# Router of a hybrid diffusion layer: a memset and a cast moved, one top-k replacement dropped, half of a modulation on another engine, gate rows copied earlier

## What is computed

```python
mod = silu(cond) @ w_mod + b_mod                       # sh1, sc1, g1, sh2, sc2, g2
mixed = (gate_a * (o_a @ w_up_a) + gate_b * (o_b @ w_up_b)) @ w_out
x = layer_norm(ALPHA * x + g1 * mixed, ln1_g, ln1_b)
u = layer_norm(x) * (1.0 + sc2) + sh2                  # modulated by set: samples, prompt
probs = softmax(u @ w_router)                          # 16 experts
aff, idx = top_k(swapaxes(probs, 1, 2), cap)           # cap 64 of samples, 16 of prompt
xs = u[idx]
hid = silu(xs @ w_gate) * (xs @ w_up)
x = layer_norm(ALPHA * x + g2 * scatter_add(hid @ w_down * aff), ln2_g, ln2_b)
```

## Time and profile before

| what | us |
|---|---|
| median of 3 runs | 1477.09 (1476.99 to 1477.68) |
| the profiled execution | 1476.4 |
| its span | 1474.6 |
| TensorE busy | 1371.4 (93%) |
| VectorE busy | 620.1 (42%) |
| ScalarE busy | 249.5 (17%) |
| GpSimd busy | 71.3 (5%) |
| mean granted TensorE clock | 0.973 |

### The profile page before, as it was taken

The page is one execution under the profiler, slowest core; times in us unless marked ns, Lnnn a source line. Parts: engine busy times, 40 slices in busy tenths (PEclk is TensorE's granted clock), DMA queues, the critical chain, the costliest instruction groups (busy, mean ns, idle before and its releaser), DMA issues.

```text
span 1474.6 us, 24328 instructions
## 1 busy us (share of the span) xinstructions
PE 1371.4 (93%) x10632; PEld 753.1 (51%) x10632; DVE 620.1 (42%) x1358; ACT 249.5 (17%) x479; POOL 71.3 (5%) x63
## 2 busy tenths in 40 slices
PE   6999999998999999999999984999999999999991
PEld 2455555657888885666755441334334334334330
DVE  6222137546666662543332774222233222222336
ACT  4311122234222332110110022000100000001000
POOL 0000000000000000000000001111111111111110
PEclk9999999999999999999999996999999999999995
DMA  9822221410000000430132055999999999999974
GB/s 387 348 104 114 81 76 71 172 56 18 2 2 2 2 17 0 171 142 31 57 129 86 30 228 216 350 393 392 397 400 403 400 396 395 398 397 387 402 304 153
DMA packets 32028, 298.93 MB, mean 203 GB/s; under 512 B 3435, under 2 KB 7659, under 8 KB 15580
## 3 DMA queue, kind: packets, MB, share of 16 engines
q1 hardware_dynamic: 20876, 270.93, 45.7%
q0 software_dynamic: 7680, 17.11, 4.6%
q10 hardware_dynamic: 3408, 9.96, 1.7%
HBM read 280.69 MB, written 17.30 MB: 202 GB/s over the span
## 4 chain that ended last, share of the span: by engine, by line
PE 64%; DVE 5%; DMA 1%; issue 1%; ACT 0%; DVEq 0%; POOLq 0%
PE bank L570 62%; PE bank L991 1%; DVE hbuf L1884 1%; DVE front L1654 0%; DVE hbuf L2034 0%; DVE stats L2032 0%; PE bank L997 0%; DVE front L1999 0%; DMA hbuf<-y_dram 0%; DMA y_dram<-front,misc 0%; DMA front<-u_dram,misc 0%; DVE misc L1935 0%; PE bank L511 0%; DVE misc L1933 0%; DVE front L1936 0%
## 5 line engine op out<-in xcount | busy, mean ns | idle before, releaser
L570 PE MATMUL bank<-ring,front 128*32 128x256 f32 (+3 forms) x3312 | 430.6, 458 | 2.2 <-DVE front L1990 2.2
L570 PE MATMUL bank<-front,ring 128*128 128x128 f32 (+3 forms) x1416 | 402.9, 443 | 6.9 <-DVE front L1843 3.0
L570 PEld LDWEIGHTS bank<-front,ring 128*128 128x128 f32 (+1 forms) x1416 | 223.3, 189 | 187.0 <-issue 163.8
L570 PEld LDWEIGHTS bank<-ring,front 128*32 128x32 f32 (+3 forms) x3312 | 177.2, 124 | 248.6 <-issue 211.2
L570 PE MATMUL bank<-front 128*64 128x512 f32 (+4 forms) x3008 | 288.4, 355 | 4.4 <-DVE front L1714 2.4
L570 PEld LDWEIGHTS bank<-front 128*128 128x128 f32 (+3 forms) x3008 | 170.1, 141 | 107.5 <-issue 79.4
L2014 DVE TENSOR_TENSOR front<-bank,front 128x512 f32<-128x512 f32 x16 | 11.1, 692 | 275.2 <-PE bank L570 275.2
L1999 DVE STREAM_TRANSPOSE front<-front 32x256 f32<-32x256 f32 x192 | 83.4, 434 | 5.5
L1443 DVE SCALAR_TENSOR_TENSOR front<-bank,pk,front 128x511 f32<-128x511 f32 x64 | 32.2, 545 | 99.4 <-ACT front L1078 98.8
L1654 DVE COPY_PREDICATED front<-ck,bank 128x256 f32<-128x256 uint32 (+1 forms) x120 | 52.8, 443 | 25.3 <-PE bank L570 22.9
L1270 ACT ACTIVATE front<-bank 128x512 f32<-128x512 f32 x16 | 9.6, 597 | 291.6 <-PE bank L570 291.6
(11 more groups left out here) (290 smaller groups left out, 988.8 us busy)
## 6 DMA issues: line engine op xcount, KB each, us to landing
ring<-w_e_gate_dram SPq DMA_DIRECT2D x32, 2048.0 KB, 15.5
ring<-w_e_up_dram SPq DMA_DIRECT2D x32, 2048.0 KB, 14.5
front<-w_e_down_dram SPq DMA_DIRECT2D x32, 2048.0 KB, 14.9
ring<-w_in_dram SPq DMA_DIRECT2D x11, 2048.0 KB, 8.0
ring<-w_mod_dram SPq DMA_DIRECT2D x10, 2048.0 KB, 12.8
front<-w_mod_dram SPq DMA_DIRECT2D x2, 2048.0 KB, 29.1
ring<-w_out_dram SPq DMA_DIRECT2D x2, 2048.0 KB, 9.6
h_spill<-hbuf ACTq DMA_DIRECT2D x1, 2560.0 KB, 16.3
```

The costliest lines, as they stand in the source:

```text
L570: return pe.matmul(out, lhsT, rhs, start=(k == 0), stop=(k == n - 1))
```

## The change

It has five pieces.

- The four copies of the g1 rows stand ahead of `gate_sums(4)` now, not behind `gate_sums(7)`.
- The prompt's modulation is split: VectorE does the blocks 0 to 3, ScalarE the blocks 4 to 7.
- The samples' row of logits (128x512) is copied by ScalarE, the prompt's (128x128) still by VectorE.
- In the last of the eight rounds of the top-k the replacement is left out.
- The memset of `xg` stands ahead of the wait for the transposed probabilities; the cast to `gather_row` stands in the middle of the lane work.

```diff
@@ scalar
             modulate(u2T, "xn2T_mm", "u2T", 32, 24, {2: lambda: root1(ST, 0), 6: lambda: root1(ST, 1)})
+            act.wait_ge(sem("xn2T_mm_prompt"), 2)
+            for k in range(4, KB):
+                A(u2T[:, k, SEQ_S:TOK], bank[1][:, P * (k - 4):P * (k - 4) + P], ACT.Identity, bias=modT[:, 72 + k:73 + k],
+                  scale=modT[:, 80 + k:81 + k]).then_inc(sem("u2T_prompt"), 1)
+            act.wait_ge(sem("router_mm"), 1)
+            A(lrow[:, 0:SEQ_S], bank[4][:, :], ACT.Copy).then_inc(sem("logit_row"), 1)
             act.wait_ge(sem("logits"), 4)
@@ vector
-            def modulate_prompt(dst, mm_done, out, sc, sh):
+            def modulate_prompt(dst, mm_done, out, sc, sh, blocks=range(KB)):
...
                 if n == 4:
+                    for c in range(2):
+                        dve.wait_ge(sem("spread_mm"), c + 1)
+                        for j in range(2):
+                            V.tensor_copy(grow[:, c, 512 * j:512 * j + 512], bank[SPREAD_BANKS[0][2 * c + j]][:, :]).then_inc(sem("gate_row"), 1)
+                    dve.wait_ge(sem("gate_row"), 4)
                     s.settle()
                     gate_sums(4)
...
                     gate_sums(7)
-                    for c in range(2):
-                        dve.wait_ge(sem("spread_mm"), c + 1)
-                        for j in range(2):
-                            V.tensor_copy(grow[:, c, 512 * j:512 * j + 512], bank[SPREAD_BANKS[0][2 * c + j]][:, :]).then_inc(sem("gate_row"), 1)
-                    dve.wait_ge(sem("gate_row"), 4)
...
-            modulate_prompt(u2T, "xn2T_mm", "u2T_prompt", 32, 24)
+            modulate_prompt(u2T, "xn2T_mm", "u2T_prompt", 32, 24, range(4))
 
             dve.wait_ge(sem("router_mm"), 1)
-            V.tensor_copy(lrow[:, 0:SEQ_S], bank[4][:, :]).then_inc(sem("logit_row"), 1)
...
             s = Stage("topk")
+            s.add(V.memset(xg[64:96, :], 0.0))
             s.add(V.memset(rrow[2 * E:3 * E, SEQ_C:HALF], -1.0))
...
-                s.add(V.match_replace(rrow, top_list[:, eight], rrow, -1.0))
+                if r + 1 < CAP_S // 8:
+                    s.add(V.match_replace(rrow, top_list[:, eight], rrow, -1.0))
...
                 s.add(V.tensor_copy(lane_aff[:, 0, c], top_value[:, 0:CAP_S]))
+            dve.wait_ge(sem("token_tr"), 1)
+            V.tensor_copy(gather_row[0:CAP, :], bank[7][0:CAP, 0:E]).then_inc(sem("gather_row"), 1)
             s.add(V.tensor_copy(lane_rows[:, 1, :], C("lane_row")[0:16, :]))
...
             V.engine_nop().then_inc(sem("lane_row"), 1)
-            dve.wait_ge(sem("token_tr"), 1)
-            s.add(V.memset(xg[64:96, :], 0.0))
-            s.settle()
-            V.tensor_copy(gather_row[0:CAP, :], bank[7][0:CAP, 0:E]).then_inc(sem("gather_row"), 1)
             s.add(V.memset(xcT, 0.0))
```

More of the change, by code:

```diff
@@ L1416, in _ @@
             mod_column(3)
-            def modulate_prompt(dst, mm_done, out, sc, sh):
-                for k in range(KB):
+            def modulate_prompt(dst, mm_done, out, sc, sh, blocks=range(KB)):
+                for k in blocks:
                     dve.wait_ge(sem(mm_done + "_prompt"), 1 + k // 4)
```

## The result

The changed kernel takes **1471.03 us** (median of 6 runs, 1468.13 to 1472.64), the kernel before, run beside it, 1477.04 (6 runs, 1474.54 to 1478.62). The ratio is 0.9957, interval 0.9947 to 0.9968: faster by 0.4%, 6.0 us between the medians. The forecast was 1471.5, range 1469.8 to 1473.9, from a sum of 5.57 us.

A forecast was written before the change was run, and what follows sets the result against it. The expert loop runs at TensorE's pace, so its start, set by the router's hand-over chain and an earlier TensorE wait, decides. Gains of 2.98 + 0 + 0.30 + 0 + 0.39 + 1.90 = 5.57 us from 1477.09 gave 1471.5, range 1469.8 to 1473.9.

The forecast's parts named there:

- Part 1: Matmul stretch before the router: copying gate rows ahead of the sums removes TensorE's wait, gain 2.98 us, at least 2.5.
- Part 2: Prompt's modulation before the router product: splitting it over VectorE and ScalarE gains 0, up to 0.7 us at the higher clock.
- Part 3: Logit copies behind the router product: ScalarE copying the samples' row gains 0.30 us (0.1 to 0.5), table load costing nothing.
- Part 4: Gather tile's memset, moved into VectorE's wait for the transposed probabilities: cost 0 there, with 0.4 us of cover to spare.
- Part 5: End of the top-k, between last search and cast: leaving out the eighth replacement gains 0.39 us.
- Part 6: Cast that feeds the gather: it starts earlier, without lane rows and memset ahead, gaining 1.90 us (0.9 to 2.0).
- The price of the lower clock: Start of the expert loop: 4.3 us at half speed cost 2.2 us, staying the same in both kernels.
- the 0.7 us allowed for the clock: Whole kernel: 0.7 us added on both sides of the range, because the clock's edges may fall otherwise.
- (a): Rival: the router gives back its share while the gate rows' gain holds, 1475.1 or 1474.1 us; chance 0.08 for both.
- (b): Rival: another wait replaces the gate rows' wait before the router, leaving 2.59 us of gain, 1474.5 us; chance 0.04.
- (d): Rival: on the router's chain the logit copy or cast comes no earlier, 1474.1 us; chance 0.04.
- (c): Rival: the gather runs into the weight transfers and may take 14.8 us longer, 1486.3 us; chance 0.04.

The follow-up runs named there:

- experiment 2: The changed kernel with the gate rows' copies put back behind the gate sums: 1474.81 us, ratio 0.9979.
- experiment 1: The kernel before with only the gate rows' copies moved ahead of the gate sums: 1472.60 us, ratio 0.9964.
- experiment 4: The changed kernel with the cast to the gather's row back behind the lane rows, the memset staying moved: 1469.45 us (one run).
- experiment 10: The changed kernel with the first expert's last two weight blocks waiting for the list's transposes instead of the router: 1477.64 us, ratio 1.0008.
- experiment 8: The changed kernel with the second gates' spread behind the probabilities' transposes, both top-k memsets ahead of the router's wait, and fillers, short gaps included: 1465.1 us, ratio 0.9908.
- experiment 9: The changed kernel, order of work untouched, with fillers in TensorE's idle times, short gaps included, none before the probabilities: 1465.5 us, ratio 0.9918.

## Why the prediction was right, step by step

**Part 1** gave 3.36 us in the trace for 2.98 forecast. The copies lie where the working put them. Its size came out low twice. The wait's recorded length alone was taken, and the stretch gained 0.38 beyond it. Rows account for most of that: the gates' groups of eight matmuls are recorded at 2.32 us but follow each other every 2.15 (754.66, 756.81 before), so the wait that is recorded as 2.98 kept the next block 3.15 us from its turn, 0.17 more; and the first gate sum starts 2.52 us behind its product's start instead of 2.41, so the stretch begins 0.11 later, which shortens it and is no gain. The last 0.10 is open. And that TensorE may lose its higher clock behind such a wait (2.96 us in experiment 2) was not in the term at all. It may be what lifts experiment 1's 4.8 us above the trace's 3.36. The clock's column would have said so much: in the trace of before it is lower in stretches of the first half too (453.6 to 457.1, 494.6 to 498, 535.6 to 539 us), so a fall was to be reckoned with outside the router as well.

**Part 2** was rightly 0 where the lower clock rules and 0.65 at the higher, for 0.5 worked out. The term in the result is -0.34, by the clock's edge. Before, the lower clock ran from 873.5 to 876.9 and its first 0.5 us fell on an idle TensorE, ahead of the transposes of 873.99. After, it runs from 872.1 to 875.5, all of it on work: the transposes (from 870.94) took 1.09 us instead of 1.97, but the samples' product behind them 4.06 instead of 2.83. The mechanism (the clock and not the modulation decides there) was named, its edge could not be.

**Part 3** gave 0.29 for 0.30. The exp's table was no obstacle:

```profile
876.70 1.28 ACT L1262 ACT_TABLE_LOAD   x1
...
878.68 0.27 ACT L1262 ACTIVATE dec<-dec 128x80 f32<-128x80 f32 x1 [0.69 <-DVE dec L1920]
```

The exp starts 1.98 us after the load's start, released by VectorE. The Trainium skill, ScalarE: Activation LUTs, section What ACT_TABLE_LOAD costs, puts load and drain together at about 2.66 us; by that, an estimate, the exp would start at 879.36 at the earliest. The trace disagrees: the exp started 0.68 us before that.

**Part 4** cost nothing, as forecast, but with 0.1 us of cover in place of 0.4. The step that failed is the cover's: it counted the idle time and the memset, and not the 0.27 us before a memset starts. A second tile of that size would already have cost 0.99 of the 1.23 us that the memset's move brings.

**Part 5** gave 0.37 for 0.39. **Part 6** gave 1.98 for 1.90. The Trainium skill, SBUF — State Buffer, section SBUF: two separate sides, has VectorE's fp32 copies within SBUF hold up the gather's descriptors. In experiment 4 the copies between cast and issue cost nothing (1.00 against 1.01 us). But while GpSimd issued (896.91 to 897.87) VectorE made no such copy, so these runs do not test the rule for that stretch.

**The loop's start.** The price of the lower clock stayed, as the sum said, but the first turn is 0.27 longer: it starts 5.3 us earlier, and the higher clock comes back at 909.7 instead of 914.4, so 4.9 us at the lower level in place of 4.3. This the 0.7 us allowed for the clock took in.

**The total.** That the traces' 5.30 comes so near the sum of 5.57 is in part luck: the 0.38 us too little in part 1 and the 0.34 of part 2 cancel. And between runs that lie 4.5 us apart a median within 0.5 us of the forecast says little about the single terms; the table does.

**The rivals.** (a), (b) and (d) are excluded by the table: each part's gain stands in the stretch where it was made, and experiments 1 and 2 give both halves by themselves. (c) exists, its price was sized wrong. The step was the loop's median landing of 18.7 us, taken as what a gather costs beside weights; in the loop it meets standing traffic, in experiment 10 two blocks and the rows behind them, and is used after 10.4. What makes the rest of the loop's 18.7 no run shows. With 6.1 us in place of 14.8 the rival would have stood at 1471.5 + 6.1 = 1477.6, not slower by more than can be told, so its 0.04 belonged to "same".

## What to carry to other kernels

When a wait lies between long matmul stretches, price it with the clock: what TensorE loses is the wait and, in some runs, the lower clock behind it; look in the trace whether other waits of that length were followed by a fall. Where engines hand over to each other in steps of a microsecond, filler products that keep TensorE busy were worth more (4.0 us between the medians, 3.1 in the traces) than most reorderings, but each must end before the work that it guards, at the lower clock too. And a move into idle time is covered only by what is left after the moved operation's own start: here 0.1 us of an idle stretch of 1.3.

## What the hardware showed that was not expected

- A wait of 2.98 us is followed by the lower clock in one trace (experiment 2) and by the higher in another (before), with the same instructions around it.
- The changed kernel's six runs go from 1468.13 at a mean clock of 0.977 to 1472.64 at 0.973. Part of such a spread is there before any filler or router edit: in the twelve traces the first gate sum starts between 698.25 and 702.00 us, and the lower clock comes at different places ahead of it (535.6 to 539 us before, not in the changed kernel; 373 to 378 us in the changed kernel, not before). So traces are better compared stretch by stretch than by their ends.
- One filler of 384 columns in each of two gaps of 1.0 to 1.3 us, with the late spread and one more filler ahead of the probabilities, went with a clock that stayed up (experiment 8); the same two without these did not (experiment 9, lower from 890.0 to 896.8). Just ahead of the fall TensorE had been idle for 1.85 us in experiment 9 and for 0.86 at the same place in experiment 8. Which of these differences decides, these runs don't settle. The two lines, experiment 8 first:

```profile
890.29 0.26 PE L946 MATMUL bank<-ck,misc 48*128 48x48 f32 x1 [0.86 <-DVE misc L1957]
...
889.60 0.26 PE L945 MATMUL bank<-ck,misc 48*128 48x48 f32 x1 [1.85 <-DVE misc L1955]
```

- A memset of 32x1024 starts 0.16 to 0.27 us after the operation ahead has ended, where the memset of 16x128 behind it follows after 0.08 and the product ahead of it (879.47, behind 879.25 for 0.19) after 0.03.
